# One hybrid decoder layer: the four value tiles of an expert step multiplied in four column groups, their buffers given back together

## The reference

```python
eidx = jnp.take_along_axis(cidx, fi, axis=-1)          # (token, 8 heads, 16 experts)
g = jax.nn.softmax(fv, axis=-1)
act = jax.nn.gelu(jnp.einsum("td,trkd->trk", xc, u_tab[eidx]).astype(jnp.float32))
return jnp.einsum("trk,trkd->td", (g * act).astype(xc.dtype), v_tab[eidx])
```

## Time and profile before

| | |
|---|---|
| median of 3 runs | 2758.88 us |
| the profiled execution, own time | 2762.28 us |
| its span, first to last instruction | 2760.5 us |
| PE busy | 1943.0 us (70%) |
| DVE busy | 1145.6 us (41%) |
| POOL busy | 950.1 us (34%) |
| queue of the gathers | 671.13 MB, 59.6% of the 16 engines' time |
| all DMA, mean over the span | 320 GB/s |
| PE in L1774, 2560 records | 662.2 us |

### The profile page before, as it was taken

One profiled execution on the slowest core, in us unless ns is written; L12 is line 12 of the kernel. 1 busy time (PEld: TensorE's weight loads), 2 busy tenths in 40 slices (PEclk: granted clock), 3 DMA queues, 4 the chain that ended last, 5 costly groups with the idle time before them and its releaser, 6 DMA issues.

```text
span 2760.5 us, 20809 instructions
## 1 busy us (share of the span) xinstructions
PE 1943.0 (70%) x8059; PEld 911.6 (33%) x8059; DVE 1145.6 (41%) x2076; ACT 270.7 (10%) x642; POOL 950.1 (34%) x644
## 2 busy tenths in 40 slices
PE   7999999998846567868788645454444443578777
PEld 3444454454642226523246411111111111122224
DVE  1000043112136754544523456656556565544442
ACT  1000001111012212110010000000000000000002
POOL 0000000000025644342242455656556555545540
PEclk9999999997977786679888867676777677799989
DMA  7463233422649999899899999999999999999998
GB/s 242 125 218 122 97 105 121 156 95 100 233 174 422 421 367 377 347 382 366 345 400 356 384 395 421 421 397 422 397 421 421 394 419 394 387 418 415 416 418 299
DMA packets 211414, 884.20 MB, mean 320 GB/s; under 512 B 25496, under 2 KB 49944, under 8 KB 126651
## 3 DMA queue, kind: packets, MB, share of 16 engines
q0 software_dynamic: 92160, 671.13, 59.6%
q1 hardware_dynamic: 118586, 208.70, 22.1%
q10 hardware_dynamic: 576, 3.15, 0.4%
HBM read 870.91 MB, written 12.95 MB: 320 GB/s over the span
## 4 chain that ended last, share of the span: by engine, by line
PE 51%; DMA 35%; POOL 4%; DVE 3%; issue 3%; ACT 2%; SPq 1%; DVEq 0%; PEldq 0%; ACTq 0%; POOLq 0%
DMA arena<-in_peer_v,arena 25%; PE bank L1774 15%; PE bank L1415 12%; PE bank L1465 4%; POOL arena L591 4%; PE bank L1420 3%; DMA arena<-in_peer_wq 2%; DMA arena<-in_w_out 2%; PE bank L1593 2%; PE bank L1569 2%; DMA arena<-in_peer_u,arena 2%; PE bank L1725 2%; PE bank L1829 2%; DMA arena<-in_state_win 1%; PE bank L1705 1%
## 5 line engine op out<-in xcount | busy, mean ns | idle before, releaser
L1774 PE MATMUL bank<-arena 128*32 128x512 f32 x2560 | 662.2, 725 | 655.5 <-DMA arena<-in_peer_v,arena 585.8
L1296 DVE CUSTOM_DVE_ANT_0 arena<-arena 128x2048 f32<-128x2048 f32 x320 | 731.5, 2292 | 683.4 <-DMA arena<-in_peer_u,arena 651.8
L586 POOL DMA_INDIRECT arena<-in_peer_u,arena x320 | 455.9, 1425 | 932.5 <-DVEq L1277 814.5
L591 POOL DMA_INDIRECT arena<-in_peer_v,arena x320 | 494.0, 1544 | 801.8 <-PE bank L1774 743.0
L1774 PEld LDWEIGHTS bank<-arena 128*32 128x32 f32 x2560 | 171.9, 130 | 1122.9 <-issue 1056.9
L1415 PE MATMUL bank<-arena 128*128 128x512 f32 (+2 forms) x800 | 326.2, 567 | 7.1 <-PE bank L1420 5.8
L1415 PEld LDWEIGHTS bank<-arena 128*128 128x128 f32 (+1 forms) x800 | 147.4, 198 | 176.7 <-issue 176.6
L1465 PE MATMUL bank<-arena 128*128 128x285 f32 x256 | 123.5, 658 | 0.9 <-DVE arena L1019 0.6
L1829 PE MATMUL bank<-arena 128*128 128x512 f32 x256 | 112.7, 595 | 0.0
L860 ACT ACTIVATE arena<-arena 128x4 f32<-128x4 f32 x80 | 16.4, 205 | 954.9 <-DVE arena L1296 954.7
L1725 PE MATMUL bank<-arena 128*128 128x192 f32 x512 | 91.4, 343 | 16.1 <-DMA arena<-in_peer_wq 16.1
(11 more groups left out here) (199 smaller groups left out, 1423.9 us busy)
## 6 DMA issues: line engine op xcount, KB each, us to landing
arena<-in_w_in SPq DMA_DIRECT2D x22, 2048.0 KB, 7.8
arena<-in_w_out SPq DMA_DIRECT2D x8, 2048.0 KB, 8.6
arena<-in_peer_wq SPq DMA_DIRECT2D x8, 2048.0 KB, 8.0
arena<-in_w_out SPq DMA_DIRECT2D x16, 1024.0 KB, 16.2
arena<-in_peer_wq SPq DMA_DIRECT2D x16, 1024.0 KB, 20.1
arena<-in_ple_gate SPq DMA_DIRECT2D x32, 512.0 KB, 15.0
arena<-in_ple_gate SPq DMA_DIRECT2D x8, 2048.0 KB, 14.1
arena<-in_cache_kv SPq DMA_DIRECT2D x64, 128.0 KB, 2.6
```

The lines of the kernel that those rows point to most:

```text
L586: pool.indirect_dma_start(u_row[j], None, I["peer_u"][0], bass.IndirectOffsetOnAxis(idx[:, i, c + j:c + j + 1], 0)).then_inc(u_in[j], 16)
L591: pool.indirect_dma_start(v_row[j], None, I["peer_v"][0], bass.IndirectOffsetOnAxis(idx[:, i, c + j:c + j + 1], 0)).then_inc(v_in[j], 16)
L1296: dve.tensor_tensor_reduce(out=u_row[j], in0=u_row[j], in1=n_rep[rep_of(i)[0]], scale=1.0, scalar=0.0, op0=ALU.mult, op1=ALU.add, accum_ou ...
L1774: ins = pe.matmul(bank[q][32 * j:32 * j + 32, :], diag[:, k % 2, j, :], v_row[j][:, 512 * q:512 * q + 512], start=(s == 0), stop=(s == SST ...
```

## The change

PE waits for all four value tiles of a step before it starts on any of them. It then goes through the four column pieces, and in each through the four tiles, so that matmuls of four different column groups follow each other. `v_used` rises once a step, by 4, after the last of the 16 matmuls. POOL waits once, before the first `v` gather of the next step, for that rise, and issues the other three without a wait. The number of matmuls and gathers, their sizes and all other waits stay as they are.

```diff
@@ POOL
             for j in range(4):
-                if k:
-                    pool.wait_ge(v_used, 4 * (k - 1) + 2 * (j // 2) + 2)
+                if k and j == 0:
+                    pool.wait_ge(v_used, 4 * k)
                 pool.indirect_dma_start(v_row[j], None, I["peer_v"][0],
@@ PE, weighted_rows
-            for j0 in (0, 2):
-                for j in (j0, j0 + 1):
-                    pe.wait_ge(v_in[j], 16 * (k + 1))
-                for q in range(4):
-                    for j in (j0, j0 + 1):
-                        ins = pe.matmul(bank[q][32 * j:32 * j + 32, :], diag[:, k % 2, j, :], v_row[j][:, 512 * q:512 * q + 512],
-                                        start=(s == 0), stop=(s == SSTEP - 1))
-                ins.then_inc(v_used, 2)
+            for j in range(4):
+                pe.wait_ge(v_in[j], 16 * (k + 1))
+            for q in range(4):
+                for j in range(4):
+                    ins = pe.matmul(bank[q][32 * j:32 * j + 32, :], diag[:, k % 2, j, :], v_row[j][:, 512 * q:512 * q + 512],
+                                    start=(s == 0), stop=(s == SSTEP - 1))
+            ins.then_inc(v_used, 4)
```

## The result

The changed kernel takes 2874.28 us, the median of 4 runs (2871.95 to 2886.75), against 2759.14 us before: 1.0426 times, 95% interval 1.0396 to 1.0457. It is 115 us slower, outside the range of 2742 to 2776. The profiled execution took 2886.75 us with a span of 2885.0.

A forecast was written before the change was run, and what follows sets the result against it. The prediction took the DMA stream's bytes to bound the steady steps. Early bursts gave -8.6 us, late gathers +3, sum -5.6 from 2758.88: 2753.3, said as 2753.5 us (chance 0.50), range 2742 to 2776.

The forecast's parts named there:

- What bounds the kernel: Steady steps, 1672 to 2312 us: DMA bytes set the pace, 8.39 MB a step at 420 GB/s, 20.0 us.
- Four groups at once in 8 slots: PE's value products: four groups run together, burst 3.65 us at full clock, 4.94 to 6.60 us in steady steps.
- rival D: Value products on PE: four groups do not run at once in this order; +84 us, 2843; chance 0.05.
- E: Value products on PE: four groups run at once, but a slot gets longer; 2768 us; chance 0.03.
- The time of the give-back: POOL's first value gather is issued 3.0 to 4.6 us (the lead) before the stream ends at the fourth u tile.
- A: From the landing of a step's fourth value tile to the next step's first value gather issue: 5.3 to 7.0 us.
- What lead is needed: Steady steps: the first value gather must be issued 2.9 to 4.0 us before the u rows end.
- B: From a step's first value gather issue to the landing of its fourth value tile: at least 5.4 + 7.5 us.
- rival C: Steady steps: buffers come back too late and the queue runs dry; priced at 14 us, 2769; chance 0.15.
- So they stay ahead if the first does: POOL's later gathers keep ahead of the stream if the first does: third and fourth 4.0 and 6.4 us behind it.
- The three us of loss: Steady steps: total loss from the later first gather, put at 3 us between nothing and some 14 us.
- The early bursts: Six bursts before 1600 us, all four tiles landed long before: 1.73 us shorter each, 10.4 us, net 8.6 us gained.

The follow-up runs named there:

- Half dots: Changed kernel; from step 36 to 61 DVE's row products cover 1024 of 2048 columns: 2834.92 us.
- half dots before the change: Kernel before; from step 36 to 61 DVE's row products cover half of the columns: 2763.95 us against 2762.17.
- alone the edit: Kernel before, with the change only in the 14 steps where PE reaches its products after all four tiles have landed: 2769.91 us against 2760.38, ratio 1.0040.

## Why the prediction was wrong

*What bounds the kernel: right.* Inner steps as long as their bytes, 20.0 us; every kernel with a lead of 8 us or more stayed at 20.0 to 20.2.

*Four groups at once in 8 slots: right.* 3.64 us at full clock (3.65 forecast), 5.05 to 6.53 us in the steady steps (4.94 to 6.60), 440.6 us in all. Rivals D and E are out. The Trainium skill's rule of strict program order ("TensorE: Matmul & The Clock Gate", Part 3, "What overlaps and what doesn't") does not hold in the way I had read it: at 16 slots of 0.427 us a full-clock burst would take 6.8 us, and it is over in 3.64.

*The time of the give-back: right.* A lead of 3.0 to 4.6 us was forecast; it is 3.1 to 5.3 us, 3.7 on the mean. A was forecast at 5.3 to 7.0 us and is 6.1.

*What lead is needed: this step failed.* I put "the time from issue to landing in an empty queue less the 2.49 us in which the bytes flow", 2.9 to 4.0 us, and took the end of the stream to be the landing of the fourth u tile. The runs show 20.12 us at 5.9, 21.45 at 4.7, 22.39 at 3.7: about 6 us are needed in an inner step. In the loop's terms, the prediction had 5.4 + 7.5 = 12.9 us for B (in its rival D), and B is 15.9 to 16.4 us in the five kernels in the table whose issues stand beside whole row products and whose lead is 3.7 to 5.9 us. With 12.9 the loop closes in 19.0 us and hides behind the bytes; with 16.3 it takes 22.4. By the prediction's own sign, a share below one with loads in fours, this is rival C.

The 5.4 us was the least time to landing in the whole trace, taken for the usual one; the first gather takes 7.6 us on the mean here. That alone makes the lead needed 5.1 us by the same formula. Two more things were missed:

The landing of a tile is no end of the stream. Between the first issue at 1738.42 and 1740.4 the changed kernel's engines are nearly idle, though the fourth u tile is not there before 1741.5:

```profile
1738.40:1740.40 2.00, 0.87 (x5) 0.48 (x4) 1.84 (x3) 0.77 (x2) 1.67 (x2) 1.00 0.18 74
1740.50:1742.00 1.50, 0.00 (x0) 0.00 (x0) 1.35 (x3) 0.00 (x0) 1.50 (x1) 0.58 0.75 235
```

This step is one of the drier ones. On the mean of the 18 inner steps the share is 1.01 until 4 us before that landing, 0.61 in the third microsecond before it and 0.22 in the second. In a full queue the sixteen engines drift apart; the sixteen increments of a tile's semaphore spread over 3.9 us on the mean in the kernel before, and the fourth u tile's over 2.4 us in the changed one. The Trainium skill ("DMA: Bandwidth & Descriptors", "Why a DMA increments its semaphore by 16 and not by 1") says that the engines of one transfer finish independently and only the full 16 means that all has landed; this case agrees.

"So they stay ahead if the first does" was wrong too. I had seen the issues 2.1 us long in the earlier trace rows beside row products, and not asked what stands beside them after the move. The first took 1.78 us on the mean (0.94 before), the second and third 2.2 and 2.1. Half dots take 1.5 us off B: the first gather's time to landing goes from 7.6 to 7.1 us and the three gaps behind it from 8.5 to 7.6. The Trainium skill ("SBUF — State Buffer", "SBUF: two separate sides") describes a trap of this kind: while DVE runs an instruction in a two-port mode, for which it names a 32-bit copy, POOL can't write the descriptors of a DMA that it issues. It does not name the row product of this kernel; the long issues beside it, 2.1 us in place of 0.94, look like that trap. Half dots show that their length hangs on the row products; by what mechanism, no run here shows. What the runs do show is when it matters: with half dots before the change, with a full queue, nothing was won.

*The three us of loss* became 2.35 us in an inner step, and 102.6 us in steps 0 to 7 and 28 to 63. So rival C had the mechanism, and its size, "14 us by the upper bound", was wrong sevenfold.

*The early bursts:* 10.4 us of PE time were there, the 8.6 us net were not. In the changed kernel steps 8 to 21 gave 3 us, and alone the edit gave none.

*The last stage*, put at "nothing", lost 19 us (125.8 - 106.7 from step 63 to 79). I had read the full share as protection there; a full share says that the queue is fed, not by how much. No edit was tried in that stage, so that the same loop costs the time there is likely and not shown.

*The ends of blocks*, put at "nothing" as well, lost too: the last step of a block and the first of the next together take 50.6 to 53.4 us in place of 45.9 to 47.4.

No version tried beats the kernel before.

## What to carry to other kernels

A DMA share of 1.0 tells how busy the queue is, not how far it is from running dry. Before moving a give-back later, close the loop once by hand: last landing to first issue, plus first issue to last landing, and take the second part with the issues as slow as they will be beside their new neighbours. Here a concurrency gain on an engine that waited for its data was worth less than the buffers that it held meanwhile.

## What was not expected of the hardware

- Four column groups with 32-bit floats run fully side by side (3.64 us against a forecast 3.65, for 16 matmuls of 128x32 by 128x512), although the two passes of a matmul, next to each other in program order, share a group.
- In one column group after the other, all data there, PE overlapped part of the work all the same: 8.86 us, where 16 matmuls one by one, at two passes of 0.427 us each, would take an estimated 13.7.
- The first 1 MB gather behind a nearly dry queue took 7.6 us to land on the mean, against 5.3 us for the quickest value gather in the whole trace of the changed kernel.
- An issue of a gather on POOL takes 0.94 us alone and 2.1 to 2.6 us beside a 2.29 us row product on DVE, and leaving out half of the row product took nothing off a step with a lead of 8.9 us and 1.6 us with one of 3.7.
